# Sample states of the odd layer, sequence by sequence, cut into quarters

## The reference, cut to what matters

```python
y = y + jnp.einsum('btgn,bgepn->btgep', cf, state) * jnp.exp(cum)[..., None]
to_end = jnp.exp(cum[:, -1:] - cum) * dt
new_state = (state * jnp.exp(cum[:, -1])[..., None, None]
             + jnp.einsum('bsge,bsgn,bsgep->bgepn', to_end, bf, xf))
```

## Time and profile before

| | |
|---|---|
| median of 3 runs | 3138.88 us (3135.44 to 3143.42) |
| the profiled execution | 3140.68 us, its span 3139.0 us |
| busy TensorE / its weight loads | 2773.5 us (88%) / 2197.3 us (70%) |
| busy VectorE / ScalarE / GpSimd | 1481.5 us (47%) / 769.2 us (25%) / 521.2 us (17%) |
| `sample_states` | some 138 us, from 1971.5 to 2110 us of the span |

### The profile page before, as it was taken

One profiled execution on the slowest core, in us unless ns is written; L12 is line 12 of the kernel. 1 busy time (PEld: TensorE's weight loads), 2 busy tenths in 40 slices (PEclk: granted clock), 3 DMA queues, 4 the chain that ended last, 5 costly groups with the idle time before them and its releaser, 6 DMA issues. The chain is left out here.

```text
span 3139.0 us, 40165 instructions
## 1 busy us (share of the span) xinstructions
PE 2773.5 (88%) x16275; PEld 2197.3 (70%) x16275; DVE 1481.5 (47%) x2481; ACT 769.2 (25%) x1452; POOL 521.2 (17%) x419
## 2 busy tenths in 40 slices
PE   5999898997968989979996899667999995799899
PEld 5998566675847987769996677435555543599677
DVE  4997666665311006535564400457776743100363
ACT  3221354332202213323222211112212111112231
POOL 1012000341301210222120000002121211022012
PEclk9999899997989999989998899687999997999899
DMA  3111012760031124112221221564333203211431
GB/s 108 55 34 48 14 35 80 289 237 20 1 121 61 47 88 162 54 27 80 91 85 56 83 97 42 153 210 113 101 87 94 71 4 112 70 47 41 154 123 54
DMA packets 235639, 270.71 MB, mean 86 GB/s; under 512 B 36502, under 2 KB 190678, under 8 KB 230243
## 3 DMA queue, kind: packets, MB, share of 16 engines
q1 hardware_dynamic: 215650, 179.85, 19.0%
q0 software_dynamic: 16384, 75.77, 6.8%
q10 hardware_dynamic: 3456, 12.98, 1.0%
HBM read 226.66 MB, written 41.28 MB: 85 GB/s over the span
## 5 line engine op out<-in xcount | busy, mean ns | idle before, releaser
L297 PE MATMUL pp<-HH,WS_part 128*128 128x352 f32 x1776 | 573.8, 323 | 0.0
L295 PE MATMUL pp<-HH,WH 128*128 128x352 f32 x1344 | 436.5, 325 | 40.1 <-POOL WS_part L434 40.1
L296 PE MATMUL pp<-HT_part,WH 128*128 128x352 f32 x1344 | 434.4, 323 | 0.0
L297 PEld LDWEIGHTS pp<-HH,WS_part 128*128 128x128 f32 x1776 | 336.4, 189 | 0.0
L295 PEld LDWEIGHTS pp<-HH,WH 128*128 128x128 f32 x1344 | 254.3, 189 | 42.1 <-POOL WS_part L434 42.1
L2747 PE MATMUL OP<-oWO,YT 128*128 128x512 f32 (+1 forms) x576 | 252.5, 597 | 3.3 <-DVE XE L2874 3.3
L296 PEld LDWEIGHTS pp<-HT_part,WH 128*128 128x128 f32 x1344 | 254.5, 189 | 0.0
L434 POOL TENSOR_TENSOR WS_part<-WS,WH 128x1024 fp32r<-128x1024 f32 x56 | 143.3, 2559 | 650.1 <-ACT WH L385 650.1
L2211 DVE COPY HT<-zT 128x512 f32<-128x512 f32 x64 | 44.2, 691 | 437.0 <-DMA xown<-c_batch 385.3
L2747 PEld LDWEIGHTS OP<-oWO,YT 128*128 128x128 f32 (+1 forms) x576 | 103.8, 182 | 144.0 <-issue 140.3
L1048 DVE SCALAR_TENSOR_TENSOR CV<-GXP,cw,CV 128x512 f32<-128x512 f32 x240 | 161.9, 740 | 0.0
(11 more groups left out here) (503 smaller groups left out, 5214.4 us busy)
## 6 DMA issues: line engine op xcount, KB each, us to landing
WS<-x_w_qg SPq DMA_DIRECT2D x32, 512.0 KB, 4.0
WO<-cache_mem_k SPq DMA_DIRECT2D x16, 1024.0 KB, 5.0
WO<-cache_mem_v POOLq DMA_DIRECT2D x16, 1024.0 KB, 5.5
CBt<-cum_scratch SPq DMA_DIRECT2D x8, 2048.0 KB, 10.1
xbc_scratch<-oACC ACTq DMA_DIRECT2D x24, 528.0 KB, 2.7
WS<-o_w_in SPq DMA_DIRECT2D x24, 512.0 KB, 3.8
XT<-xbc_scratch SPq DMA_DIRECT2D x8, 1536.0 KB, 7.6
WS<-e_w_in SPq DMA_DIRECT2D x18, 512.0 KB, 3.9
```

Of the source, the lines that this page charges most:

```text
L295: nc.tensor.matmul(out, wh, xh, start=start, stop=False)
L296: nc.tensor.matmul(out, wh, xl, start=False, stop=False)
L297: return nc.tensor.matmul(out, wl, xh, start=False, stop=stop)
```

## The change

The loops are written out, and a sequence is cut into quarters of four 128-column blocks. The eight banks are now: two (`TPp`) for turned states, two (`UP`) for updates, both used in turn by quarters, and four (`ACC`), one for each group, in which inter(b) of all eight sequences is summed by TensorE itself. For that C is laid out once as `CMB`, with zeros outside the sequence's tokens, in place of the mask on VectorE. The update's mask moves from `XE` (2048 columns) to `BT` (512 columns, `BM`). Decay and addition become one operation for each 128 columns, since the decay is now a per-partition scalar. States have three buffers, `SBT` two. The loads of `WO` all go behind the last state load, and the wait for them goes to the first output projection.

```diff
-                    if first:
-                        pe.wait_ge(r_w, 64)
-                    else:
+                    if not first:
...
+                for b in range(NB):
+                    if b >= 3:
+
+                        sp.wait_ge(f_un, 4 * (b - 2))
+                    sp.dma_start(SB[b % 3][:], s_in[b]).then_inc(f_l[b % 3], 16)
                 w_out = A["o_w_out"][0].rearrange("(k p) n -> p k n", p=P)
...
+                for a in range(4):
+                    sp.dma_start(WO[:, 4 * a:4 * a + 4, :], w_out[:, 4 * a:4 * a + 4, :]).then_inc(r_w, 16)
...
+                def turn(b, q):
+                    if q == 0:
+                        pe.wait_ge(f_l[b % 3], 16 * (b // 3 + 1))
+                    i = 4 * b + q
+                    if i >= 2:
+
+                        pe.wait_ge(f_te, i - 1)
+                    for k in range(4):
+                        t = nc.tensor.transpose(TPp[i % 2][:, k * P:(k + 1) * P], SB[b % 3][:, 4 * q + k, :], ident[:])
+                    t.then_inc(f_tp, 1)
+
+                def inter(b):
+                    pe.wait_ge(f_te, 4 * b + 4)
+                    for g in range(4):
+                        m = nc.tensor.matmul(ACC[g][0:SMP, :], CMB[:, g, b, :], SBT[b % 2][:, g * 512:(g + 1) * 512],
+                                             start=b == 0, stop=b == NB - 1, skip_group_check=True)
+                    m.then_inc(f_yi, 1)
+
+                def update(b, q):
+                    if q == 0:
+                        pe.wait_ge(f_xm, b + 1)
+                    i = 4 * b + q
+                    if i >= 2:
+
+                        pe.wait_ge(f_un, i - 1)
+                    for k in range(4):
+                        m = nc.tensor.matmul(UP[q % 2][:, k * P:(k + 1) * P], XE[:, (4 * q + k) * P:(4 * q + k + 1) * P],
+                                             BM[b % 2][:, q, :], start=True, stop=True)
+                    m.then_inc(f_up, 1)
...
+                for q in range(4):
+                    turn(0, q)
+
+                pe.wait_ge(dve_own.sem, d0 + 7)
+                for b in range(NB):
+                    for q in range(4):
+                        if b + 1 < NB:
+                            turn(b + 1, q)
+                        update(b, q)
+                        if q == 0:
+                            inter(b)
...
+                for b in range(NB):
+                    ins = N.tensor_copy(CMB[:, :, b, TS * b:TS * b + TS], XT[:, NX + 4:NX + 8, TS * b:TS * b + TS])
+                v(ins)
                 v(N.tensor_tensor(te[:], ce[:], CUt[0:SMP, NQ, :], ALU.subtract))
-                v(N.memset(YS[:], 0.0))
...
+                def masked(b):
+                    if b >= 2:
+
+                        dve.wait_ge(f_up, 4 * (b - 1))
+                    N.tensor_scalar(BM[b % 2][:], BT[:], bm[:, b:b + 1], None, ALU.mult).then_inc(f_xm, 1)
+
+                masked(0)
+                for b in range(NB):
+                    if b + 1 < NB:
+                        masked(b + 1)
+                    if b >= 2:
+
+                        dve.wait_ge(f_s[b % 2], 16 * (b // 2))
+                    for q in range(4):
+                        dve.wait_ge(f_up, 4 * b + q + 1)
+                        for k in range(4 * q, 4 * q + 4):
+                            ins = N.scalar_tensor_tensor(out=NW[b % 2][:, k, :], in0=SB[b % 3][:, k, :], scalar=DE[:, k, b:b + 1],
+                                                         in1=UP[q % 2][:, (k - 4 * q) * P:(k - 4 * q + 1) * P], op0=ALU.mult, op1=ALU.add)
+                        ins.then_inc(f_un, 1)
+                dve.wait_ge(f_yi, NB)
+                for g in range(4):
+                    ins = N.tensor_copy(YS[:, g * 512:(g + 1) * 512], ACC[g][0:SMP, :])
+                v(ins)
```

More of the change, by code:

```diff
@@ L3069, in turn @@
[L3069 to L3079, removed]
-                    for g in range(4):
-                        m = nc.tensor.matmul(BK[1 - s][g][0:SMP, :], XT[:, NX + 4 + g, :], SBT[:, g * 512:(g + 1) * 512],
-                                             start=True, stop=True)
-                    m.then_inc(f_yi, 1)
-                    pe.wait_ge(f_xm, b + 1)
-                    for k in range(NX):
-                        m = nc.tensor.matmul(BK[s][k // 4][:, (k % 4) * P:(k % 4 + 1) * P], XM[s][:, k * P:(k + 1) * P],
-                                             BT[:, k // 4, :], start=True, stop=True)
-                    m.then_inc(f_up, 1)
-                    if not last:
-                        pe.wait_ge(f_yo, 1 + b + 1)
-                        turn(b + 1, 1 - s, step + s)
@@ L3094, in _ @@
-                turn(0, 0, 0)
-                with loop(pe, 0, NB // 2 - 1) as j:
-                    for s in range(2):
-                        batch(2 * j + s, s, j)
-                batch(NB - 2, 0, NB // 2 - 1)
-                batch(NB - 1, 1, NB // 2 - 1, True)
+                    t = nc.tensor.transpose(UP[0][0:SMP, g * P:(g + 1) * P], XT[:, NX + g, :], ident[:])
+                t.then_inc(f_xt, 1)
+                for q in range(4):
+                    turn(0, q)
+                pe.wait_ge(dve_own.sem, d0 + 7)
@@ L3158, in _ @@
-                ready(0, 0)
-                batch(0, 0, 0)
-                batch(1, 1, 0)
-                with loop(dve, 1, NB // 2 - 1) as j:
-                    dve_own.enter(j - 1, 2)
-                    for s in range(2):
-                        batch(2 * j + s, s, j)
-                    dve_own.leave(NB // 2 - 2)
-                batch(NB - 2, 0, NB // 2 - 1)
-                batch(NB - 1, 1, NB // 2 - 1, True)
+                def masked(b):
+                    if b >= 2:
+                        dve.wait_ge(f_up, 4 * (b - 1))
+                    N.tensor_scalar(BM[b % 2][:], BT[:], bm[:, b:b + 1], None, ALU.mult).then_inc(f_xm, 1)
```

94 lines of the change are left out of this document (29 added, 65 removed).

## The result

The changed kernel takes 3111.14 us (median of 4, 3104.45 to 3117.46) where the kernel before takes 3140.78 on the same chip (median of 4, 3135.44 to 3143.42). The ratio is 0.9907, interval 0.9881 to 0.9934, so 29.2 us of gain (3140.78 x 0.0093), between 20.7 and 37.4. The forecast was 3104, with 3097 to 3123 as its range. The profiled execution of the changed kernel took 3117.46 us, its span 3115.6.

The account below looks back on a forecast made before the run. Bound: a TensorE-led ring with copy waits and a falling clock. Loop 73.4 + 2 + 2 + 1.2 = 78.6 us, new states 36.4 us sooner, less 1.5 for the late store: gain 34.9, forecast 3104 us, range 3097 to 3123.

Parts of the forecast that it names:

- a ring: Stage's loop: turn, copy, inter, update, turn over all eight banks, TensorE the largest part; copy waits 17.8 us in eight.
- handoffs: Loop's 32 quarters with two waits each: 0.13 us where just met, 0 to 4.2 us in all, 2 taken.
- a slow start: First sequence on TensorE at 1.2 GHz: 2 us if half is slow, 5.4 if all; 2 taken.
- The start: Loop starts at about 1987.4: first turn moves ahead of `XE`, which is ready 1.0 us sooner.
- The banks' slack: Update banks: 1.94 us between an update's end and the next into its bank, against VectorE's 1.1 and two handoffs.
- The thin margin of the loads: State loads: wanted 8.2 us after being asked for, landing in 6.5; margin 1.6 us.
- The late store: Stage's end: last store lands beside `WO`'s loads, making the end 0 to 3.9 us later; 1.5 taken.
- the empty queue near 2072: Transfers: some 12 MB from about 2040 are through near 2072, when the last store, asked for at 2067, should be landing.
- The clock's: Rival in the loop: clock keeps falling, every inter 5.32 us, loop 13.6 us longer, 3118; chance 0.2.
- the case of all at 1.2 GHz: Clock rival's extreme: all TensorE loop work slow, 115.0 us, total 3144, no change that can be told; chance 0.02.
- `WO` did not come late: Rival judged here: `WO` lands at 2101, first chunk's loads at 2113, a gain of 12 us, 3127; chance 0.1.
- Lock step: Rival: updates wait until VectorE has read the other bank too, 1.6 us more a quarter, about 3154; chance 0.03.

Follow-up runs that it names:

- the next trace: Changed kernel run again with no edit: median of 4 3115.71 us, ratio 0.9906 to the kernel before; stage 111.3 us.
- the unbroken order: Changed kernel with each sequence's four turn quarters together, then inter, then its four update quarters: stage 123.6 us, 12.1 us a sequence.
- the other trace of before: Kernel before profiled once more with no edit: 3145.73 us, stage 147.3 us, chunks 495.5 us.
- the order by twos: Changed kernel with turns and updates dealt out in pieces of two transposes and two update matmuls: 3147.72 us, stage 144.8 us.
- `WO` in six parts: Changed kernel with the `WO` load split into six parts of 1 or 2 MB behind state loads 2 to 7: 3116.75 us, stage 107.8 us.
- More waits: Changed kernel with one more already met wait on TensorE ahead of turn and update quarters: 3121.15 us, stage 108.4 us.
- halves: Changed kernel with two turn quarters, then two update quarters, in turn: 3118.32 us, stage 105.0 us, 9.55 us a sequence.
- the last version: Changed kernel with turn and update quarters in pairs, `WO` in six parts and last inter ahead of last updates: median of 6 3119.66 us, ratio 0.9931.

## Why the prediction was right, and where its sizes were off

**What bounds the stage** held: a ring in which TensorE waits for the copies, with the clock as a part of the price. With it broken there is no wait for ScalarE, and in the first trace inter takes 3.62 us everywhere and the clock is 1.00.

**The sequence.** The mechanism was right, the term "handoffs" was not. The forecast took 2 us for 32 of them and a period of 9.4 to 9.7. Measured are 10.23 us, and the runs show that waits cost nothing (60 more of them: still 10.23), while each change of kind costs 0.16 (to turns) or 0.18 (to updates): 28 pairs of 0.34 and two of 0.18 at the end (behind the last inter and behind the one wait), 9.9 us. That this was not 7.9 us of error is luck, and comes from the other side of the sum: I added busy times (1.97, 3.62, 3.83), in each of which a group's end is counted that the next group overlaps, and in turn and update one change of kind besides (before, an update takes 3.77 us by starts, which is 4 x 0.90 + 0.18 but for 0.01; the lines are below). By starts and without the changes the work is 28 x 0.43 + 8 x 3.55 + 32 x 0.90 = 69.2 us, not 73.4. And the 2 us for a slow start were not needed in this trace; in the next it cost 3.2. So 69.2 + 9.9 + 0.3 of waiting are 79.4, and 1.2 for VectorE give 80.6 (measured 80.7), where the forecast had 78.6. TensorE of the kernel before, an update and the turn behind it:

```profile
1999.44 3.83 PE L3086 MATMUL fU<-fBT,fXM 32*128 32x128 f32 x32
2003.21 1.97 PE L3073 MATMUL fV<-ident,fSB 128*128 128x128 f32 x16
```

**The start.** Loop from 1986.8 where the forecast had 1987.4; with the stage begun 1.2 us sooner in this trace that is 0.6 late. `XE`, taken as 1.0 us sooner, was 0.45 sooner after the stage's start (begun at 1984.05 for 1985.68). The last new state comes 33.7 us sooner after the stage's start, not 36.4.

**VectorE.** 1.1 us for a quarter was taken and 1.12 measured; it is the bound nowhere. The banks' slack was as worked out: a quarter of VectorE is done 0.55 us before the next arrives. The sum in a bank mattered more than its 2.7 us: put back, it cost 12.6 in one trace, by a wait and the clock behind it.

**The transfers.** The thin margin of the loads held (6.7 us to land, and no turn in the loop waited for `fSB`; in the next trace one did, 1.42 us); taken away it costs 48 us and the whole gain. The late store was mis-sized: 1.5 us taken, 3.6 measured (2.1 to 3.8 over four traces: 9.74, 11.12, 11.31 and 11.5 against 7.67). The store lies beside 414 GB/s of `WO`, and with `WO` elsewhere the tail is 7.3. It is 7.3 as well in the unbroken order, where `WO` stands behind the last state too but has landed by 2085.1, before the last new state at 2087.5. The step that was wrong is the empty queue near 2072: `WO` lasted until 2078, since the transfers went at 370 GB/s over the end of the loop where 422 had been taken (27 us become 31). The Trainium skill ("DMA: Bandwidth & Descriptors", section "Issuing engines are not separate DMA queues") has all queues interleave on the same 16 engines, by which the forecast had worked out 3.9; three of the four traces of this order (3.4 to 3.8) agree with that, not with my discount; the fourth has 2.1.

**The sum.** 34.9 us of gain were forecast, and the stage shows 30.0: 2.7 missing in the loop and its start and 2.1 in the tail. The whole time shows 29.2, with an interval wide enough for both; that and a median of before that lies 1.9 us higher than the one I started from make the 7 us between 3104 and 3111. That the stage and the whole agree so closely is luck in part: against the other trace of before, with its stage of 147.3, the stage gains 38.9, and the chunks took back 8 to 11 us in two of the three traces of the changed kernel.

**The rivals.** The clock's was no fancy: the unbroken order brings it down without any idle over 0.39 us (stage 123.6), the order by twos without any idle, and a wait of 1 us does so in four cases of seven (5.17 for one inter behind). Inside the loop of the changed order it didn't fall; at the loop's two ends it did in the second trace (5.84 and 5.05 for inter) and with `WO` in six parts (5.32 and 4.96). Two prices of this rival were misread. An update at 4.6 us is not one at 1.2 GHz throughout, for it began fast: in the unbroken order half an update took 3.70 us slow, at 2082.68, where it takes 2.05, so that a wholly slow update would take some 7 us (an estimate from this), and the case of all at 1.2 GHz would have been some 20 us beyond 3144. And the updates are two fifths of the 73.4 us (30.6), not a third. `WO` did not come late: its last part landed by 2078 and the first `CBt` 14.1 us after its issue, under the 15 that I had named. Lock step did not occur.

**What stays open.** Why a change between the two kinds costs 0.17 us; the weight load of the next group begins with the group, but no run here took one away. Why the order by quarters keeps the clock where twos and whole runs lose it. And which form the chunks take: they had the long form (some 507) in two of three traces of the changed kernel and in neither of two of the kernel before. The nine other traces have the chunks' code of the changed kernel too, but for the count of one wait in two of them. More waits, halves and `WO` in six parts had 506.9 to 507.1, the other six 495.0 to 501.4. The five long ones are just those whose chunks began between 2076 and 2082 us of the span; of the traces without it none did. So the long form may go with the time at which the stage ends, and a part of the gain be paid back there, but no run here was made to show it.

## What to carry to other kernels

Add up TensorE by start-to-start times, and price each change of kind by itself: cut a ring only as finely as its latencies ask, since halves were 0.68 us a sequence cheaper than quarters and twos 1.4 dearer. Where a stage's mean clock is under 1, look at what stands behind each wait, and try more than one order of the kinds, for here neither the longest runs nor the shortest kept the clock; 2.2 us of waiting went from each sequence and nearly 4 us were won. Before moving a large load, look at what lands beside it at both places, the last store of a stage above all.

## What the runs showed of the hardware that was not expected

- The clock falls under matmuls with no idle to speak of. With four quarters of update in a row, nowhere over 0.39 us idle, the mean was 0.77, and by twos, with no idle at all ahead of the last update, 0.73; the same instructions had 1.00 by quarters (0.95 in the trace in which TensorE waited for the second state) and 0.95 by halves (in the last version, with one late state). The Trainium skill ("TensorE: Matmul & The Clock Gate", section "Part 1: The HAM clock gate (the "warmup" mystery)") has the clock gated by idleness and released by sustained work; the waits of 1.72 and 7.99 us with slow matmuls behind agree with it, and so do four of the seven waits of 1.03 to 1.62; the fall at 1997 to 2010 in the unbroken order and the falls inside the loop by twos do not, taken so simply.
- A change between 128-row turns and 32-row updates costs 0.16 to 0.18 us at the full clock. A semaphore wait that is already met costs nothing that the trace shows.
- The same code takes 495 to 507 us in the chunks and the kernel before 138.5 or 147.3 us in this stage, with another pattern of the clock in each. A comparison of spans from one trace each was off by 6 us from the ratio of the medians.
